# Two U rows gathered behind each of tile 0's first V batches, and the engines' steps in another order

## The reference: one layer with attention, a delta rule and retrieved experts

```python
def peer(h, w_pq, sub_keys, expert_u, expert_v):
    q = (hf @ w_pq).reshape(T, PEER_HEADS, 2, PEER_DK // 2)
    s = jnp.einsum('thpd,hpnd->thpn', q, sub_keys).astype(jnp.float32)
    sv, si = lax.top_k(s, PEER_TOPK)
    cand = (sv[:, :, 0, :, None] + sv[:, :, 1, None, :]).reshape(T, PEER_HEADS, PEER_TOPK * PEER_TOPK)
    ...
    top_s, pos = lax.top_k(cand, PEER_TOPK)
    eidx = jnp.take_along_axis(cidx, pos, axis=-1).reshape(T, PEER_HEADS * PEER_TOPK)
    gates = jax.nn.softmax(top_s, axis=-1).reshape(T, PEER_HEADS * PEER_TOPK)
    act = jnp.einsum('td,nd->tn', hf, expert_u)
    a_sel = jnp.take_along_axis(act, eidx, axis=1).astype(jnp.float32)
    coef = (gates * jax.nn.gelu(a_sel, approximate=False)).astype(h.dtype)
    dense = jnp.zeros((T, N_EXPERTS), h.dtype).at[jnp.arange(T)[:, None], eidx].add(coef)
    return (dense @ expert_v).reshape(B, S, D)
```

## Time and profile before

| | |
|---|---|
| median of 3 runs | 1316.68 us (1314.01 to 1317.79) |
| profiled execution | 1318.91 us, span 1317.0 us |
| PE, DVE, ACT, POOL busy in the span | 1003.0, 874.8, 295.5, 560.7 us |
| DMA | 492.55 MB, mean 374 GB/s |
| mean granted clock of PE | 0.92 |

### The profile page before, as it was taken

How to read it: one execution, slowest core, us unless ns; L and a number is a source line. 1 busy time by engine, 2 the same in 40 slices (tenths; PEclk the granted TensorE clock), 3 DMA queues, 4 the chain that set the end, 5 groups by cost and what they waited for, 6 DMA issues and landing times.

```text
span 1317.0 us, 15195 instructions
## 1 busy us (share of the span) xinstructions
PE 1003.0 (76%) x5204; PEld 591.7 (45%) x5204; DVE 874.8 (66%) x2295; ACT 295.5 (22%) x760; POOL 560.7 (43%) x599
## 2 busy tenths in 40 slices
...
DVE  0536249899973889523799604896779666665665
...
DMA  9988368699999999999999999999999999999995
GB/s 383 365 314 321 152 224 321 236 334 412 365 408 386 328 401 379 380 376 353 373 402 410 410 409 411 396 422 421 422 421 419 421 422 421 422 422 421 421 422 233
DMA packets 96683, 492.55 MB, mean 374 GB/s; under 512 B 10720, under 2 KB 11616, under 8 KB 68192
## 3 DMA queue, kind: packets, MB, share of 16 engines
...
HBM read 488.93 MB, written 2.62 MB: 373 GB/s over the span
## 4 chain that ended last, share of the span: by engine, by line
PE 37%; DMA 25%; DVE 22%; POOL 6%; issue 6%; ACT 3%; POOLq 0%; SPq 0%; DVEq 0%; ACTq 0%
PE bank L1295 34%; DMA wring<-in_euv,consts 20%; DVE big L2164 7%; POOL big L860 4%; DVE extra L2164 2%; DVE wring L2164 2%; PE bank L1301 1%; PE bank L1324 1%; DVE ops L2164 1%; DMA big<-in_ev,consts 1%; DVE W L2188 1%; DMA big<-in_euv,consts 1%; ACT hT L951 1%; DMA big<-in_eu,idx 1%; DVE hT L2164 1%
## 5 line engine op out<-in xcount | busy, mean ns | idle before, releaser
L1295 PE MATMUL bank<-big,W 128*32 128x512 f32 (+1 forms) x932 | 298.5, 653 | 82.5 <-DVE W L2188 56.9
L2164 DVE CUSTOM_DVE_ANT_0 big<-big,hnow 128x1024 f32<-128x1024 f32 x226 | 269.6, 1217 | 70.9 <-DMA big<-in_euv,consts 63.3
L1295 PE MATMUL bank<-wring,W 128*128 128x512 f32 (+1 forms) x456 | 176.5, 635 | 68.4 <-DVE W L2188 67.7
L1295 PEld LDWEIGHTS bank<-big,W 128*32 128x32 f32 (+1 forms) x932 | 103.8, 156 | 242.8 <-issue 236.6
L870 POOL DMA_INDIRECT big<-in_euv,consts x113 | 106.9, 946 | 151.2 <-PE bank L1295 143.6
L2164 DVE CUSTOM_DVE_ANT_0 wring<-wring,hnow 128x1024 f32<-128x1024 f32 x90 | 109.2, 1220 | 71.2 <-DMA wring<-in_euv,consts 68.9
L860 POOL DMA_INDIRECT big<-in_ev,rowT x119 | 112.9, 948 | 77.0 <-issue 35.2
L1295 PEld LDWEIGHTS bank<-wring,W 128*128 128x128 f32 (+1 forms) x456 | 64.5, 173 | 167.9 <-issue 165.7
L870 POOL DMA_INDIRECT wring<-in_euv,consts x76 | 71.9, 946 | 138.6 <-PE bank L1295 132.4
L1295 PE MATMUL bank<-big 128*128 128x128 f32 (+1 forms) x1056 | 115.6, 266 | 12.0 <-DVE big L1925 7.6
L1295 PEld LDWEIGHTS bank<-big 128*128 128x128 f32 (+1 forms) x1056 | 106.0, 179 | 28.1 <-issue 13.2
(11 more groups left out here) (364 smaller groups left out, 1477.6 us busy)
## 6 DMA issues: line engine op xcount, KB each, us to landing
wring<-in_wch SPq DMA_DIRECT2D x23, 2048.0 KB, 11.9
...
```

The costliest lines, as they stand in the source:

```text
L1295: return nc.tensor.matmul(out, lhsT, rhs, start=first, stop=last)
L2164: V.tensor_tensor_reduce(u, u, hnow[:, :], 1.0, 0.0, ALU.mult, ALU.add, coef[t % 2][:, n:n + 1]).then_inc(dot_ready, 1)
```

## The change

In `gather_order`, 24 U rows of tile 0's second half (`gu.0.64` to `gu.0.87`) stand two by two behind the V batches 4 to 15 of tile 0's first half. From gather 152 on the list is the same as before.

```diff
+FIRST_AMONG, AMONG = 4, 2
...
-    out = []
+    out, early = [], 0
     for t, a in HALVES:
-        out += [("gu", t, HALF * a + n) for n in range(HALF)]
-        out += [("gv", t, a, b, j) for b in range(BATCHES) for j in range(QUADS)]
+        out += [("gu", t, HALF * a + n) for n in range(early, HALF)]
+        early = 0
+        for b in range(BATCHES):
+            out += [("gv", t, a, b, j) for j in range(QUADS)]
+            if (t, a) == (0, 0) and b >= FIRST_AMONG:
+                out += [("gu", t, HALF + n) for n in range(early, early + AMONG)]
+                early += AMONG
     out += [("gw", 1, n) for n in range(HALF, SLOTS)] + [("gw", 2, n) for n in range(SLOTS - LAST)]
```

```diff
+experts.1.1.0 dot.1.0:9 take.0 dot.1.9:63 slot_gates.1.0 pair_sums.2.0.1 dot.1.63 coef.1.0 pair_sums.2.0.0
...
+spread.49 dot.2.38:45 spread.53 spread.51:53 dot.2.45:48 spread.54 dot.2.48:50 spread.55 dot.2.50:52 spread.57
```

More of the change, by code:

```diff
@@ L240 @@
[L240 to L243 removed]
+warm.0:3 mod.0 warm.3 mod.1 mod_turn.0 warm.4 mod.2 mod_turn.1:3 mod.3 x_turn.0.0 mod_turn.3 channels.0.0 channels.1.0
@@ L268 @@
-dot.0.87 head_norm.1.1 dn_p.2.0.4 dot.0.88 z_gate.1 dot.0.89:91 dn_p.2.0.5 dot.0.91:93 dn_p.2.0.6 dot.0.93:100
-resid.1.0 dot.0.100:105 resid.1.1 dot.0.105 norm.1.1 dot.0.106:108 dn_o.2.0 head_norm.2.0:2 dot.0.108 z_gate.2
-dot.0.109:117 resid.2.1 dot.0.117:128 coef.0.1 resid.2.0 norm.1.2 top_key.0.1 pair_sums.1.0.0 top_pair.1.0.0
-places.1.0.0 top_key.1.1 gate.1.0.0:2 pair_sums.1.0.1 chosen.1.0.0.0 top_key.1.2 top_pair.1.0.1 chosen.1.0.0.1
-places.1.0.1 chosen.1.0.1.0:2 experts.1.0.0 top_key.2.1 pair_sums.1.1.0 top_pair.1.1.0 dot.1.0:4 experts.1.0.1
@@ L273 @@
-dot.1.4:8 top_key.0.2 dot.1.8:11 take.0 dot.1.11:18 places.1.1.0 dot.1.18 chosen.1.1.0.0 dot.1.19:22 slot_gates.1.0
-pair_sums.2.0.1 dot.1.22:36 top_pair.2.0.1 dot.1.36:52 expert_rows.1.0 dot.1.52:64 coef.1.0 top_key.3.1
-pair_sums.1.1.1 top_pair.1.1.1 places.1.1.1 chosen.1.1.1.0:2 gate.1.1.0 experts.1.1.1 chosen.1.1.0.1 experts.1.1.0
-dot.1.64:67 pair_sums.2.0.0 top_pair.2.0.0 dot.1.67 slot_gates.1.1 dot.1.68 places.2.0.1 spread.1 spread.0 top_key.2.2
-dot.1.69:71 spread.2 dot.1.71:73 spread.3 places.2.0.0 dot.1.73:75 spread.4 dot.1.75:77 spread.5 chosen.2.0.1.0
@@ new lines @@
+expo.0.2 dn_tt.0.1.1 dn_p.0.0.2 dn_p.0.1.2 dn_tt.0.0.2 dn_tt.0.1.2 diff.0.2 dn_p.0.1.3 dn_p.0.0.3 dn_tt.0.1.3 expo.0.3
+dn_tt.0.0.3 diff.0.3 dn_p.0.0.4 dn_p.0.1.4 dn_full.0.0:2 dn_p.0.0.5 dn_p.0.1.5 dn_p.0.0.6 dn_p.0.1.6 head_norm.0.0
+dn_o.0.0:2 head_norm.0.1 gate.0.0.0 dn_s.0.0 z_gate.0 gate.0.0.1 resid.0.0:2 mod_turn.9 scales.1 norm.1.0 dn_s.0.1
+top_key.0.0 pair_sums.0.0.0 top_pair.0.0.0 places.0.0.0 channels.0.1 channels.1.1 chosen.0.0.0.0 channels.2.1
+chosen.0.0.0.1 experts.0.0.0 channels.3.1 top_key.1.0 channels.6.1 dot.0.0:3 channels.5.1 channels.4.1 dot.0.3
@@ new lines @@
+pair_sums.0.0.1 top_pair.0.0.1 channels.7.1 places.0.0.1 dot.0.4:8 channels.8.1 chosen.0.0.1.0:2 key_norm key_scale.1
+channels.9.1 experts.0.0.1 channels.11.1 channels.10.1 top_key.2.0 expert_rows.0.0 dn_scale.2.1 key_scale.2
+pair_sums.0.1.0 dot.0.8:10 slot_gates.0.0 dn_decay.2.1 dot.0.10:13 dn_scores.2.1 dn_p.2.1.0 dot.0.13:15 rope.1.0
+dot.0.15:17 dn_scale.1.0 mod_turn.11 dot.0.17:19 dn_p.2.1.1 top_pair.0.1.0 dn_p.2.1.2 top_key.3.0 dn_p.2.1.3
+dot.0.19:24 dn_qg.2.1 dot.0.24 dn_p.2.1.4 dot.0.25:28 dn_p.2.1.5 dot.0.28:43 pair_sums.0.1.1 dot.0.43:51 places.0.1.0
```

220 lines of the change are left out of this document (109 added, 111 removed).

## The result

The changed kernel takes 1364.28 us (median of 4 runs, 1361.89 to 1366.17) against 1316.16 us (4 runs); the ratio is 1.0365, with an interval from 1.0351 to 1.0379. The profiled execution has a span of 1362.6 us, 45.6 more than before. The bytes are the same (404.26 and 87.33 MB on the two DMA queues that matter, as before), and so is the number of PE's instructions (5204). What has grown is waiting, and the time that PE takes: it is busy for 1035.0 us instead of 1003.0, at a mean granted clock of 0.88 instead of 0.92.

The account below looks back on a forecast made before the run. Up to about 650 us transfers wait for engines, behind it engines wait for saturated transfers. Front -3, gathers 192 to 271 -6 and tail +3 make -6 us: 1310.5 against the median 1316.68; range 1301 to 1322.

Parts of the forecast that it names:

- the three stretches: The kernel split at gather 192 (543.83 us) and gather 271 (669.70 us); time at gather 271 was to carry to the end.
- The tail: Wide rows: spreads behind runs of dots leave three rows in flight at 11 places, 0.3 us each, 3 us lost.
- The rival that ends slower: Each of the tail's 11 places costs 1.3 us instead of 0.3, 14 us in all; 1326 to 1322 us, chance 0.13.
- DVE ahead of coef.0.0: Choices leave DVE's full 198 to 362 us: gather 192 about 3 us earlier, bounds 4 later and 8 earlier.
- The 24 U rows: Twelve dots move to 380 to 440 us, where DVE idles; gain between 0 and 8.3 us, taken at 0.
- PE behind w_out of tile 2: query.1.1 first leaves PE idle until about 552 us for its weights; cost between 0 and 9 us, taken as 2.
- DVE ahead of dot.1.0: Tile 1's choices, 20.4 us, stand ahead of its first dot, hidden by DVE's idle time in 550 to 650 us.
- Gather 192 to 271: This stretch takes 125.9 us against 118 at 409 GB/s; at most 8 us to gain, 6 taken.

Follow-up runs that it names:

- e3: Kernel before with only the steps up to about 380 us in the changed kernel's order, gather order of before: 1334.28 us, ratio 1.0134.
- e9: Kernel before with only the changed gather order, the 24 rows' dots moved behind the V batches among which they are gathered: 1330.88 us, ratio 1.0104.
- e4: Kernel before with only the steps between 540 and 823 us in the changed kernel's order: 1310.62 us, ratio 0.9948.
- e1: Changed kernel with the steps behind 823 us, where its first wide row lands, back in the order of before: 1327.58 us, ratio 1.008.
- e17: Kernel before with spreads 40 to 87 of tile 2 in threes, each behind a run of six dots: 1326.78 us, ratio 1.0083.
- e14: Kernel before with spreads 40 to 87 of tile 2 in fours, each behind a run of eight dots: 1382.5 us, ratio 1.0497.
- e2: Kernel before with only the steps behind the first wide row (813 us) in the changed kernel's order: 1374.19 us, ratio 1.0433.
- e5: Kernel of e2 with spreads and gelu steps put back in the order of their slots, runs of dots as long: 1358.17 us, ratio 1.0327.
- e8: Kernel before with only the steps up to about 205 us, the first gather, in the changed kernel's order: 1326.22 us, ratio 1.008.
- e18: Kernel of e8 with the order of before restored between about 100 and 146 us: 1322.66 us, ratio 1.0051.
- e7: Kernel before with the changed kernel's order and gather order from 357 to 823 us: 1317.02 us, ratio 1.0008.
- e12: Kernel of e4 with query.0.1 and its rest put back ahead of query.1.1 behind w_out of tile 2: 1311.98 us, ratio 0.9965.
- e16: Kernel before with only the steps between 540 and about 655 us in the changed kernel's order: 1310.93 us, ratio 0.9951.

## Why the prediction was wrong, point by point

*The frame was right.* What bounds the kernel, the three stretches, and that the start of the queue carries to the end unless the tail has bubbles. Only the mark was some 4 us off: what is gained at gather 271 carries only as far as it still stands at the first wide row. From there, e3, e9 and e4 end within 1.3 to 2.3 us of where they began (16.1 to 14.8, 15.0 to 13.6, -10.1 to -7.8), and e1 within 1.1. One reading was wrong without harm: DVE's least busy stretch of those four windows has 15.88 us of 50, not 24.94.

*The tail is the step that failed: 3 us taken, 37 measured.* The rival that ends slower was the right one, with a chance of 0.13, though its own price for the tail, 14 us, was too small as well. I counted 11 places at which 7 of ten homes are held, and gave each 0.3 us because three rows in flight would last until the first home is free. The same count has 15 more places with six held, which I left out. What the changed kernel shows at dots 38 to 44 of tile 2, first DVE:

```profile
1126.89 0.08 DVE L2171 DVE_READ_ACCUMULATOR2_ANT coef<- 128x1 f32 x1
...
1134.71 1.22 DVE L2171 CUSTOM_DVE_ANT_0 wring<-wring,hnow 128x1024 f32<-128x1024 f32 x1 [2.76 <-DMA wring<-in_euv,consts]
...
1138.00 1.22 DVE L2171 CUSTOM_DVE_ANT_0 wring<-wring,hnow 128x1024 f32<-128x1024 f32 x1 [1.52 <-DMA wring<-in_euv,consts]
```

then PE and POOL at the same place, and the windows of 5 us ahead of the pause, at its end and behind it:

```profile
1114.88 3.60 PE L1302 MATMUL bank<-wring,W 128*128 128x512 f32 x8
1128.17 6.38 PE L1302 MATMUL bank<-wring,W 128*128 128x512 f32 x8 [9.70 <-DVE W L2195]
```

```profile
1118.75 0.94 POOL L877 DMA_INDIRECT wring<-in_euv,consts  x1 [0.78 <-PE bank L1302]
1132.19 0.94 POOL L877 DMA_INDIRECT wring<-in_euv,consts  x1 [12.51 <-PE bank L1302]
```

```profile
1110.00:1115.00 5.00, 5.00 (x13) 2.21 (x12) 3.44 (x8) 0.00 (x0) 2.81 (x3) 1.00 1.01 419
1125.00:1130.00 5.00, 1.83 (x2) 0.83 (x3) 3.94 (x10) 0.20 (x1) 0.00 (x0) 0.50 1.01 419
1130.00:1135.00 5.00, 5.00 (x9) 2.21 (x8) 1.52 (x3) 0.00 (x0) 1.11 (x2) 0.64 0.44 131
```

The run ends with three spreads at once (W x6, 1126.89). PE has been without work for 9.70 us and does the first two rows in 6.38 us, where the pair ahead of that took 3.60. POOL issues nothing for 12.51 us, and DVE waits 2.76 us for the last row in flight and 1.52 for the one behind it. The rows in flight don't last: from 1130 to 1135 us the rate falls to 131 GB/s, a loss of some 3.4 us at this place alone (5 us times 290/421). Two things were missing from my price. No home comes free before the run of dots is over and its first spread is made, and PE then sums the run's rows one by one. And PE starts that at a granted clock of 0.50 (1125 to 1130 us), against 1.00 in the pair ahead, so that two rows take 6.38 us. Which of the two weighs more was not tried. By runs of one length a run costs 0.7 us for 6 dots and 5.5 for 8 (e17, e14). The measured hole that I took my bound from (2.0 us at 842.45) was a single late issue. And I didn't count the swaps, some 14 us of 57 in e2 against e5 (they hold PE at the earlier slot, in order, while the later one's matrix lies ready; that this is the reason was not tried).

The estimate that I set beside it, from the Trainium skill ("DMA: Bandwidth & Descriptors", Anatomy of one DMA), was 4.4 us for a wide row by itself. The row issued at 1132.19 met its dot at 1138.00, 5.8 us later. So it is a little short here, but that was not what failed: POOL could issue nothing for 12.51 us ahead of this row. The Trainium skill's rule for PE ("TensorE: Matmul & The Clock Gate", Part 1: The HAM clock gate) is that the slow clock is the default and activity lifts it; 6.38 against 3.60 us behind a pause of 9.70 us agrees with it. The 17 us at half clock from 113 us on, with PE busy 4.58 to 5.00 of 5 us in most of them, don't fit that rule by busy time alone.

*DVE ahead of coef.0.0: 3 us gain taken, 12.5 us late at coef.0.0 and 17.5 at gather 192 measured.* I looked for the front's price on DVE alone. The 6.4 us of choices did leave (coef.0.0 regains 5 of the 18 us that dot.0.31 is late), but what goes with PE's clock ahead of the first gather costs some 7 us of the 10.8 (8.6 in e8 less 1.2 in e18's profiled run), and the steps from 205 to 380 us cost 6 more (e3 less e8, 17.0 and 10.7). Of the two channel steps ahead of the first experts, which I feared, e8 and e18 hold one, so that it costs 1.2 us at most; the first gather of e3, which holds both, is 1.8 later than e8's. My bound of 4 us late was too narrow because it held only the mechanisms that I had named.

*The 24 U rows: 0 taken, 16 late at gather 192 measured by themselves, 5 with the steps moved along.* One half of the reasoning was right: gather 151 gains 4.9 us (e9), and that doesn't carry, since gather 192 hangs on w_out of tile 2. The other half, that later V batches only reorder PE's work, was the error: PE's batches wait for rows that now land later and hold up the attention's steps behind them, 16 us where they stay in place (e9) and 4.9 where they are moved (e7, whose other steps from 357 us on are changed too).

*PE behind w_out of tile 2: right in the pause, too dear in the price.* The pause was forecast as some 10 us, and it is 10.44. Its cost was taken as 2; e12, which puts query.0.1 first again, is no faster, so there is none.

*DVE ahead of dot.1.0: right.* From resid.2.1 (557.90) to dot.1.0 (674.27) it is 116.4 us, against 114.9 before: all but 1.5 of the 20.4 us of choices were hidden.

*Gather 192 to 271: right.* 6 us were taken and 8 called the most; it is 11.2 in the changed kernel (561.35 to 676.04) and 12.1 in e4, but 7.5 and 8.4 up to the first wide row, where the bytes that slid behind gather 271 have been moved too. The floor of 118 us counted 48.2 MB; 45.9 are moved between the two gathers in the changed kernel (400 GB/s over 114.69 us) and 47.1 before, so it was some 6 us too high.

In sum, from the experiments: 17.0 (e3), 8.1 (e7, 1.5 slower, less e4), -6.6 (e4) and 36.7 (after less e1) make 55.2 us, of 48.1 measured. They don't add up, since the first three overlap (e1, which has them all, is 10.3 slower and not 18.5).

Three versions beat both kernels: e4 and e16, 0.5% faster than before, and e12, 0.35% faster, with the changed order only from 540 us on and before's order of spreads.
